# A two-layer diffusion trunk with 32 experts: expert rows added to the token rows by the scatter itself

## The reference

```
x = x + g1 * mix
x = x + g2 * hierarchical_moe(rms_norm(x, norm2) * (1 + sc2) + sh2, lp)

# hierarchical_moe: 2 of the 8 experts of the best of 4 groups, weights p
y = sum over the token's two experts e of  p_e * (silu(h @ wg[e]) * (h @ wu[e])) @ wd[e]
```

## Time and profile before

| what | value |
|---|---|
| median of 3 runs | 1453.54 us |
| profiled execution, its own time | 1456.33 us |
| its span, first to last instruction | 1454.6 us |
| TensorE busy | 1224.5 us, 84% |
| VectorE busy | 708.0 us, 49% |
| ScalarE busy | 283.9 us, 20% |
| GpSimd busy | 114.9 us, 8% |
| DMA traffic | 334.53 MB, mean 230 GB/s |
| mean granted clock of TensorE | 0.921 |

### The profile page before, as it was taken

One profiled execution on the slowest core, in us unless ns is written; L12 is line 12 of the kernel. 1 busy time (PEld: TensorE's weight loads), 2 busy tenths in 40 slices (PEclk: granted clock), 3 DMA queues, 4 the chain that ended last, 5 costly groups with the idle time before them and its releaser, 6 DMA issues.

```text
span 1454.6 us, 19124 instructions
## 1 busy us (share of the span) xinstructions
PE 1224.5 (84%) x7062; PEld 710.8 (49%) x7062; DVE 708.0 (49%) x1543; ACT 283.9 (20%) x708; POOL 114.9 (8%) x171
## 2 busy tenths in 40 slices
PE   5999999878976788898849999988799579788782
PEld 2455545544442555565424554556345256456450
DVE  2255877672356132332353687877444623232234
ACT  0211153641121000000022104366211110000000
POOL 2000000001001111111000000000100011111100
PEclk7899999999977998999979999999999589999996
DMA  9221101356059999999760211023913299999976
GB/s 385 123 88 34 62 23 59 131 205 268 30 203 375 392 414 419 419 419 418 317 249 22 99 32 56 5 107 130 384 66 138 108 380 413 418 420 419 417 320 235
DMA packets 58174, 334.53 MB, mean 230 GB/s; under 512 B 11392, under 2 KB 11392, under 8 KB 23900
## 3 DMA queue, kind: packets, MB, share of 16 engines
q1 hardware_dynamic: 42336, 294.94, 50.1%
q0 software_dynamic: 15744, 38.34, 6.8%
HBM read 322.41 MB, written 27.61 MB: 241 GB/s over the span
## 4 chain that ended last, share of the span: by engine, by line
PE 53%; DMA 25%; DVE 9%; issue 4%; ACT 3%; DVEq 2%; SPq 2%; PEld 1%; POOL 0%; ACTq 0%; PEldq 0%; POOLq 0%
DMA U<-in_stream 13%; PE bank L1666 12%; PE bank L1604 9%; PE bank L2074 9%; PE bank L1965 7%; PE bank L2108 5%; DMA ring<-in_stream 4%; DMA RAB<-in_stream 3%; DMA RAB<-mod_rows 2%; DVE U L1214 1%; SPq L356 1%; DMA mod_rows<-RAB 1%; PE bank L1754 1%; DMA U<-moe_out 1%; PE bank L1780 1%
## 5 line engine op out<-in xcount | busy, mean ns | idle before, releaser
L2074 PE MATMUL bank<-U,HT 128*64 128x256 f32 (+2 forms) x1248 | 208.9, 407 | 32.6 <-DMA U<-in_stream 24.9
L2074 PEld LDWEIGHTS bank<-U,HT 128*64 128x64 f32 (+2 forms) x1248 | 140.4, 151 | 84.4 <-issue 59.1
L1666 PE MATMUL bank<-HT,ring 128*128 128x512 f32 (+1 forms) x640 | 175.4, 435 | 2.0 <-issue 2.0
L1604 PE MATMUL bank<-ring,HT 128*128 128x512 f32 x320 | 149.8, 610 | 6.0 <-ACT HT L609 4.2
L1666 PEld LDWEIGHTS bank<-HT,ring 128*128 128x128 f32 x640 | 97.3, 191 | 79.7 <-issue 79.7
L2074 PE MATMUL bank<-ring,HT 128*64 128x256 f32 (+2 forms) x608 | 121.0, 425 | 17.0 <-DMA ring<-in_stream 14.7
L1057 DVE SCALAR_TENSOR_TENSOR U<-U,prm 128x655 f32<-128x655 f32 x120 | 107.9, 899 | 7.3
L1965 PE MATMUL bank<-ring,HT 128*128 128x512 f32 x240 | 107.7, 598 | 0.0
L2108 PE MATMUL bank<-ring,HT 128*64 128x512 f32 (+2 forms) x224 | 95.8, 604 | 6.8 <-DMA U<-in_stream 6.8
L839 ACT ACTIVATE HT<-bank 128x256 f32<-128x256 f32 x36 | 13.8, 383 | 437.9 <-PE bank L2074 437.9
L1470 DVE TENSOR_TENSOR HT<-bank,HT 128x256 f32<-128x256 f32 x36 | 15.3, 424 | 172.4 <-ACT HT L839 172.4
(11 more groups left out here) (350 smaller groups left out, 1586.5 us busy)
## 6 DMA issues: line engine op xcount, KB each, us to landing
ring<-in_stream SPq DMA_DIRECT2D x140, 1024.0 KB, 10.5
U<-in_stream SPq DMA_DIRECT2D x108, 1024.0 KB, 21.3
RAB<-in_stream SPq DMA_DIRECT2D x18, 1024.0 KB, 21.4
U<-moe_out SPq DMA_DIRECT2D x20, 512.0 KB, 7.7
RAB<-mod_rows POOLq DMA_DIRECT2D x12, 512.0 KB, 11.9
moe_in<-CAT POOLq DMA_DIRECT2D x10, 512.0 KB, 3.7
X<-in_x SPq DMA_DIRECT2D x1, 2560.0 KB, 15.1
out_y<-X SPq DMA_DIRECT2D x5, 512.0 KB, 7.0
```

What stands on the lines that cost most here:

```text
L1604: ins = e.matmul(bank[:], HT[:, k, t * P:(t + 1) * P], wide(q, k), start=(k == 0), stop=(k == KD - 1))
L1666: ins = e.matmul(out, wt(q)[:, k, P * (n % 2):P * (n % 2) + P], HT[:, k, lo:lo + w], start=(k == 0), stop=(k == KD - 1))
L2074: ins = e.matmul(PS[2 + p][s, FF * j:FF * j + FF], xgT[:, p, k, s], wt(key)[:, k, :], start=(k == 0), stop=(k == KD - 1))
```

## The change

**Scatter.** `x_dram` (640 rows) takes the place of `moe_out`; in the last layer the output tensor itself does (`rows_of`). When a tile's second norm is done, GpSimd stores the tile of `X` there, beside the tile of `moe_in`. The scatter then adds (`compute_op=ALU.add`) the result rows to the token rows in memory. A token's two experts now meet in one row. So a scatter must not overlap another: each waits for the one before to land, across rounds too, and a P round is scattered in 2 parts and a Q round in 4, one for each expert, by index tables (`half`, `quarter`) in which the rows of the other experts are out of range. That is 8 + 16 + 8 = 32 scatters in a layer instead of 18.

**Afterwards.** `rows_back`, its 10 loads and its adds are gone. After the first layer five loads bring `X` back; after the second nothing is left but the last scatter.

**Places.** While `X` is in memory, its place on chip holds two more weight tiles (`XTILES`), 16 places instead of 14.

**Order of rounds.** The last three rounds B, P, P become P, P, B.

```diff
-ROUNDS = list("PPFPFQBPBPPFBQBBPP")
+ROUNDS = list("PPFPFQBPBPPFBQBPPB")
...
-RING, EXT, LATE_TILES = 6, 5, 3
-PLACES = RING + EXT + LATE_TILES
+RING, EXT, XTILES, LATE_TILES = 6, 5, 2, 3
+PLACES = RING + EXT + XTILES + LATE_TILES
...
+        def rows_of(l):
+
+            return y_out if l + 1 == DEPTH else x_dram
+
+        def parts_of(r):
+
+            return len(blocks[r][1])
+
+        def scattered(l, r):
+
+            same = range(r % 2, NR, 2)
+            return 16 * (l * sum(parts_of(i) for i in same) + sum(parts_of(i) for i in same if i <= r))
...
-                e.wait_ge(S["ov_go"], l + 1)
+                e.wait_ge(S["h2_st"], 32 * NT * (l + 1))
+                for i in range(RING + EXT, RING + EXT + XTILES):
+                    load_expert(i)
+                e.wait_ge(S["tables_rdy"], 3 * l + 3)
                 e.wait_ge(S["wslot_ps"], l + 1)
-                for i in range(RING + EXT, PLACES - 1):
+                for i in range(RING + EXT + XTILES, PLACES - 1):
...
-                for i in range(2):
-                    e.wait_ge(yfree[i], 16 * (NR // 2) * (l + 1))
-                for t in range(NT):
-                    for k in range(2):
-                        e.dma_start(yk[k][:, t, :], yk_dram[k * NTOK + t * P:k * NTOK + (t + 1) * P, :]
-                                    ).then_inc(yld[t], 16)
-
-            for t in range(NT):
-                e.wait_ge(S["x_rdy"], NT * (DEPTH - 1) + t + 1)
-                e.dma_start(y_out[:, t, :], X[:, t, :]).then_inc(S["out_st"], 16)
-            e.wait_ge(S["out_st"], 16 * NT)
+                for r in (NR - 2, NR - 1):
+                    e.wait_ge(yfree[r % 2], scattered(l, r))
+                if l + 1 < DEPTH:
+                    for t in range(NT):
+                        e.dma_start(X[:, t, :], x_dram[t * P:(t + 1) * P, :]).then_inc(yld[t], 16)
...
                     e.dma_start(h2_dram[t * P:(t + 1) * P, :], CAT[:, t, :]).then_inc(S["h2_st"], 16)
+                    e.dma_start(rows_of(l)[t * P:(t + 1) * P, :], X[:, t, :]).then_inc(S["h2_st"], 16)
...
                     e.wait_ge(S["y2_sb"], NR * l + r + 1)
-                    e.indirect_dma_start(yk_dram, bass.IndirectOffsetOnAxis(slots[:, n:n + 1], 0), yb[:, r % 2, :], None,
-                                         bounds_check=2 * NTOK - 1, oob_is_err=False).then_inc(yfree[r % 2], 16)
+                    if r:
+                        e.wait_ge(yfree[(r - 1) % 2], scattered(l, r - 1))
+                    m = parts_of(r)
+                    for a in range(m):
+                        if a:
+                            e.wait_ge(yfree[r % 2], scattered(l, r) - 16 * (m - a))
+                        at = gidx[:, n:n + 1] if m == 1 else half[:, a, n:n + 1] if m == 2 else quarter[:, a, n - NR + 2:n - NR + 3]
+                        e.indirect_dma_start(rows_of(l), bass.IndirectOffsetOnAxis(at, 0), yb[:, r % 2, :], None,
+                                             bounds_check=NTOK - 1, oob_is_err=False, compute_op=ALU.add).then_inc(yfree[r % 2], 16)
...
-                e.drain().then_inc(S["ov_go"], 1)
+                e.drain().then_inc(S["tables_rdy"], 1)
+                off, mid = small(200, 2, 3), small(206, 2)
+                for j in range(3):
+                    e.tensor_scalar(off[:, 0, j:j + 1], rowno[:, 0, 0:1], float(QUART * (j + 1)), float(NOROW), ALU.is_gt, ALU.mult)
+                dr()
...
+                for j in range(2):
+                    e.tensor_scalar(half[:, j, :], sf, off[:, j, 1:2], None, ALU.add)
...
-                def rows_back(t, m):
-
-                    e.wait_ge(yld[t], 32 * (m + 1))
-                    e.tensor_tensor(X[:, t, :], X[:, t, :], yk[0][:, t, :], ALU.add); dr()
-                    e.tensor_tensor(X[:, t, :], X[:, t, :], yk[1][:, t, :], ALU.add).then_inc(S["x_rdy"], 1)
```

More of the change, by code:

```diff
@@ L147, in build @@
         h2_dram = nc.dram_tensor("moe_in", (NTOK, D), F32, kind="Internal").ap()
-        yk_dram = nc.dram_tensor("moe_out", (2 * NTOK, D), F32, kind="Internal").ap()
+        x_dram = nc.dram_tensor("x_rows", (NTOK, D), F32, kind="Internal").ap()
         X = sb("X", [P, NT, D])
@@ L263, in build @@
         nrow2 = view(LATER + 4 * D, D)
-        slots = sb("slots", [P, NBLK], I32)
+        half = sb("half", [P, 2, NBLK], I32)
+        quarter = sb("quarter", [P, 4, 2], I32)
         gidx = sb("gidx", [P, NBLK], I32)
@@ L343, in tile_at @@
                 return view((s - RING) * SLOT, SLOT)
+            if s < RING + EXT + XTILES:
+                return X[:].rearrange("p t n -> p (t n)")[:, (s - RING - EXT) * SLOT:(s - RING - EXT + 1) * SLOT]
             if s == PLACES - 1:
                 return RB.rearrange("p a b -> p (a b)")
-            return view(LATER + (s - RING - EXT) * SLOT, SLOT)
+            return view(LATER + (s - RING - EXT - XTILES) * SLOT, SLOT)
+        def rows_of(l):
[5 more added lines that the diff above has]
+            return 16 * (l * sum(parts_of(i) for i in same) + sum(parts_of(i) for i in same if i <= r))
         @block.sync
@@ L408, in _ @@
                 some = e.value_load(ovn[0:1, 0:1], min_val=0, max_val=NOVF)
-                for slot in (RING + EXT, RING + EXT + 1):
+                for slot in range(RING + EXT + XTILES, PLACES - 1):
                     e.wait_ge(free[slot], 1 + max(spot[(l,) + t][1] for t in tiles if slot_of((l,) + t) == slot))
@@ L499, in _ @@
                 if l:
-                    e.wait_ge(S["x_rdy"], NT * l)
+                    for r in (NR - 2, NR - 1):
+                        e.wait_ge(yfree[r % 2], scattered(l - 1, r))
                 for v, h in ((xp, XPAD), (gp, GPAD)):
@@ L576, in _ @@
                         e.sem_inc(S["cst"], 1)
-                        e.indirect_dma_start(yk_dram, bass.IndirectOffsetOnAxis(scur, 0), yb[:, 0, :], None,
-                                             bounds_check=2 * NTOK - 1, oob_is_err=False).then_inc(S[f"ov_scatter{l}"], 16)
+                        e.indirect_dma_start(rows_of(l), bass.IndirectOffsetOnAxis(gcur[:], 0), yb[:, 0, :], None,
+                                             bounds_check=NTOK - 1, oob_is_err=False, compute_op=ALU.add).then_inc(S[f"ov_scatter{l}"], 16)
                         e.wait_ge(S[f"ov_scatter{l}"], 16 * (n + 1))
@@ L947, in _ @@
                     evac1(2)
-                    rows_back(4, l - 1)
                     norm1(3, 2)
@@ L1417, in _ @@
                 e.tensor_tensor(sf, PS[6][:, NBLK:2 * NBLK], sf, ALU.add); dr()
[L1418 to L1422, removed]
+                e.tensor_copy(gidx[:], sf).then_inc(S["tables_rdy"], 1)
                 e.tensor_tensor(place, iota[:].unsqueeze(1).to_broadcast((P, 2 * NT, P)),
@@ L1440, in _ @@
                 e.tensor_copy(ovn[:], ovf)
-                e.drain().then_inc(S["ov_go"], 1)
+                e.drain().then_inc(S["tables_rdy"], 1)
[3 more added lines that the diff above has]
+                dr()
+                e.tensor_scalar(off[:, 1, :], off[:, 0, :], -1.0, float(NOROW), ALU.mult, ALU.add); dr()
+                e.tensor_tensor(mid, off[:, 1, 0:2], off[:, 0, 1:3], ALU.add)
+                for j in range(2):
+                    e.tensor_scalar(half[:, j, :], sf, off[:, j, 1:2], None, ALU.add)
+                dr()
+                few = sf[:, NR - SMALLS // 4:NR]
+                for j, gap in enumerate((off[:, 0, 0:1], mid[:, 0:1], mid[:, 1:2], off[:, 1, 2:3])):
+                    e.tensor_scalar(quarter[:, j, :], few, gap, None, ALU.add)
                 e.wait_ge(S["wslot_ps"], l + 1)
@@ L1501, in _ @@
                 with e.If(some > 0):
-                    e.wait_ge(yfree[0], 16 * (NR // 2) * (l + 1))
+                    e.wait_ge(yfree[0], scattered(l, NR - 2))
                     with e.Fori(0, NOVF) as i:
```

41 lines of the change are left out of this document (15 added, 26 removed).

## The result

The changed kernel takes 1558.2 us (median of 4 runs, 1555.93 to 1561.33) where the kernel before takes 1455.3 on the same chip: ratio 1.0699, 95% interval 1.0671 to 1.0727. It is slower, as forecast, and inside the range, but by 103 us where the forecast said 28. The profiled execution spans 1554.2 us.

The account below looks back on a forecast made before the run. In the expert stretches the weight stream and TensorE were taken as nearly level bounds. Profiled 1456.3 us minus 22.2 (end) minus 4.2 (between layers) plus 29.2 and 26.5 (scatter chains) gave 1485.6, less 2.8 for the median: 1483; range 1425 to 1575.

Parts of the forecast that it names:

- The sum's own formula: Expert layers: links fill the stream's time at L each, the rest take s each; 29.2 and 26.5 us more.
- One part of the path: Expert rounds: `result` waits for the scatter of two rounds ago, `down` for `result`, then tile places, so the stream pauses.
- Sum L = 10.0 us: Scatter chain: one link beside the weight stream, 8.5 us landing plus extras for the add's read, request and gather.
- s = 3.6: Scatter chain: one link without the weight stream, 2.6 us landing plus the same 1.0 of extras.
- The gather, taken at 0.5: GpSimd's queue: a scatter right behind a gather is late by 0 to 3 us, 0.5 on the mean.
- the slow add: Scatter chain rival: each added row's read precedes its write, L = 12, s = 4.5, 1534 us; chance 0.32.
- The time doesn't go with the rows that are real: Scatter landing: a part with half its rows out of range takes the same 8.5 us as a whole round.
- The rule of the Trainium skill: Scatter landing: about 2.0 us fixed, rest by bytes; a 40-row part lands in 2.4 us, 32 in 77.
- The reads: Expert layers: the adds read another 5.2 MB a layer, 12.5 us at 419 GB/s.
- The end of the program: After the last scatter: final loads, adds and stores vanish, gain 22.2 us, 0.2 left for the wait.
- Between the layers: Seam after the first layer: one load instead of two and no adds, gain 4.2 us, 2.6 to 7.
- Nothing for the stores, the places and the order: Storing X, two more tile places and the new round order: taken as no cost and no gain.

Follow-up runs that it names:

- e3: Kernel before with plain scatters in 32 parts a layer, each waiting for the one ahead, old order and end: 1505.0 us against 1456.2, ratio 1.0324.
- e2: Kernel before with 18 unchained adding scatters a layer into the old table, x first stored to both its halves: 1502.6 us, ratio 1.0317.
- e8: Changed kernel with each part's request carrying only its own 64 or 32 rows: 1507.0 us against 1456.9 for the kernel before, ratio 1.0332.
- e12: e8 with plain scatters instead of adding ones: 1453.8 us against 1459.8 for the kernel before, ratio 0.9959.
- e7: e2 without the add, so plain unchained scatters and x stored twice more: 1461.9 us against 1456.9 for the kernel before, ratio 1.0028.
- e10: e7 plus a 72-row memory copy behind each scatter: 1480.7 us against 1459.8 for the kernel before, ratio 1.0137.
- e4: Kernel before with x stored, two weight tiles in its place and x loaded again, scatters plain and unchained: 1468.7 us against 1456.9, ratio 1.0069.
- e1: Kernel before with only the new order of the last rounds: 1461.0 us against 1456.2, ratio 1.0040.

## Why the prediction was right in its sign and wrong in its size

**The mechanism held.** The scatters chain, and the loss is time without the stream: GpSimd is held back by "DMA x_rows<-CAT", the rate is below 419 with gaps, and in e3 the chain costs 46 us with no add. The sum's own formula comes close to the layer when it is fed with measured links: 225.5 + (32 - 225.5 / 11.0) x 5.5 = 288.7 us from the first scatter to the last landing, where the trace has 793.2 - 504.6 = 288.6. For the second layer 219.7 + (32 - 20.0) x 5.5 = 285.8, and the trace has 1546.9 - 1259.5 = 287.4 (the last landing is 5.9 us after 1541.02). That the first fits to 0.1 us is luck: with the 19.9 us that the add took in e2 in place of 12.5 for its reads it would be 292. One part of the path was wrong: none of TensorE's waits is put down to `result`. In the rounds it waited 11.7 us for VectorE's copy ahead of `down` (line 1500), and 105.8 us for the gathers, which stand behind the scatters in GpSimd's queue.

**The step that failed is the size of one link, "Sum L = 10.0 us" and "s = 3.6".** Measured on halves, L is 11.0 and s 5.5. By the formula L alone makes 7.4 us of a layer and s then another 21.9, because it puts 11.5 links where no stream runs, in its pauses or behind it: some 58 us in both layers, most of the 75 that were missing. Put in first, s makes 18.0 and L 11.3; either way the term s was the worse one. The trace, cut where the stream ends, says it so: in the first layer 24 links beside the stream, pauses included, took 242.6 us (predicted 22.5 in 225.5), and 8 behind it 46.0 (predicted 9.5 in 34.0). The term s took the fastest landing of before, 2.6 us, and the same 1.0 us of extras; a half lands in 4.7 there and a full part in 6.1. In L the extras were 1.5 and came out as 2.5: landings of 10.1 to 10.4 beside the stream, and 0.8 us from a landing to the next request, which the sum left out although a chain pays it 32 times. The gather, taken at 0.5, shows no cost: it is issued 0.3 us behind a scatter and lies some 9 us ahead of the next, and of the first five scatters those with a gather beside them landed in 10.1 to 10.2 us and the others in 10.3 to 10.4. Of the three rivals the slow add (L = 12, s = 4.5) was nearest, 1534; it said rightly that "nothing excludes it", but whether an added row waits for its read, as it has it, no run shows. The range held the result only because it was made wide enough for this rival.

**"The time doesn't go with the rows that are real"** The earlier trace rows was nearly right beside the stream and misled: it was read as a fixed price. e8 shows that it goes with the rows named in the request, cycles of 11.0, 8.4 and 7.1 us for 128, 64 and 32.

**The rule of the Trainium skill** in "DMA: Bandwidth & Descriptors", section on the anatomy of a DMA on GpSimd's path, about 2.0 us and then by bytes, is not far off behind the stream (in e12, plain, 64-row requests land in 2.5 us there, links of 3.3 with the turn), but beside it no run comes below a link of 6.4 us. The measurement decides: this rule doesn't price a chain beside a full stream. That the engines take turns by packet, as the same page of the Trainium skill says of arbitration, would fit a landing that grows with the rows named and with the stream; no run shows turns.

**The reads** (12.5 us a layer) were too small as the price of the add in the stream's time: unchained, the add costs 19.9 us of the first layer (e2 against e7), and copies of the same size 11.6 (e10).

**The end of the program.** Predicted 0.2 us from the last landing to the end, measured 7.3 (1554.2 - 1546.9); of the 22.2 us of gain 15.1 were there. The layers were off by 60.7 us together (58.3 and 58.1 more than before instead of 29.2 and 26.5); this 7.1 is the next largest piece of the 75. Another 5.1 come of the medians: the sum took 2.8 us off for a profiled run above the median, and the changed kernel's lay 2.3 below it.

**Between the layers** 4.2 us were predicted. From the last landing to the first projection it is now 805.44 - 793.26 = 12.2 us, as forecast, and was 16.2: 4.0. Only 1.3 of them were left at the second layer's first scatter (466.3 us after the last landing, 467.6 before); why, no run shows.

**Nothing for the stores, the places and the order:** e7 and e4 bear out the first two, 0 to 5 us together; the order costs 5 us by itself (e1), and what it does in the changed kernel was not run.

None of the versions tried that compute the whole output beats the kernel before. The nearest with adding scatters is e8, 50 us behind it. Even if its chain were free, the unchained add alone costs 41 us (e2 against e7), and all that the end and the seam between the layers gave back is 19.

## What to carry to other kernels

Price one link of a chain of transfers in full, its landing, the turn to the next issue and the request itself, once beside the load and once without it: here the links without the stream, the ones that looked cheap, were off the most, 5.5 us for 3.6. And look at what stands behind the chain in the same queue, here the gathers. A request costs mostly by the rows it names, so parts cut by an out-of-range index each pay for nearly the whole; cut the request instead. What an add in memory costs is not in the profile's MB; look for it in the queue's share of time and in what the stream loses.

## What the runs showed of the hardware

- An adding scatter of 128 rows takes GpSimd 1.55 to 1.63 us to issue in the changed kernel (1.0 plain). Unchained (e2) it lands in 10.1 us on the median and 4.7 at the least, where a plain one has 8.4 and 2.6 (e7).
- Adding, the queue takes 15.5% of the engines for 7.83 MB (e2) where a plain one takes 10.4% for 8.02 (e7).
- Rows out of range cost nearly what real ones do beside the stream: a half in a 128-row request takes a cycle of 11.0 us, the same as the 128-row requests that e8 keeps for one expert, and 8.4 in a request of 64 (e8). Every 128-row request makes 144 packets, whatever its rows (e3).
- GpSimd issues the next transfer 0.7 to 0.8 us after the landing it waits for (changed kernel).
- Where the program ends in a GpSimd transfer, 7.3 us lay between its landing and the end (changed kernel, one profile).
